# Second feed-forward opening block by block, activations stored in two groups, and down's activations loaded in five parts

## What is computed

```python
def _swiglu(u, w_gate, w_up, w_down):
    return (jax.nn.silu(u @ w_gate) * (u @ w_up)) @ w_down

h = x + 0.5 * _swiglu(_rms_norm(x, ffn1_norm), ffn1_w_gate, ffn1_w_up, ffn1_w_down)
...   # mixer, cross-attention
h = h + 0.5 * _swiglu(_rms_norm(h, ffn2_norm), ffn2_w_gate, ffn2_w_up, ffn2_w_down)
y = _rms_norm(h, final_norm)
```

## Time and profile before

| | |
|---|---|
| three runs | 2101.51, 2096.09, 2102.85 us, median 2101.51 |
| profiled execution | 2094.95 us |
| its span, from first to last instruction | 2093.2 us |
| TensorE matmul busy | 2038.1 us (97%) |
| VectorE, ScalarE, GpSimd busy | 1430.3 (68%), 634.3 (30%), 1230.0 us (59%) |
| mean granted TensorE clock | 0.993 |

### The profile page before, as it was taken

One profiled execution on the slowest core, in us unless ns is written; L12 is line 12 of the kernel. 1 busy time (PEld: TensorE's weight loads), 2 busy tenths in 40 slices (PEclk: granted clock), 3 DMA queues, 4 the chain that ended last, 5 costly groups with the idle time before them and its releaser, 6 DMA issues.

```text
span 2093.2 us, 24457 instructions
## 1 busy us (share of the span) xinstructions
PE 2038.1 (97%) x9194; PEld 1668.7 (80%) x9194; DVE 1430.3 (68%) x1602; ACT 634.3 (30%) x977; POOL 1230.0 (59%) x799
## 2 busy tenths in 40 slices
PE   8999999999999999999999999998999999999996
PEld 4887888888878787888877888787788888887885
DVE  7688867766777979653242555457777767787788
ACT  5422322333434500002121223234223223244452
POOL 6489988797545533122333421136799999984551
PEclk9999999999999999999999999999999999999998
DMA  7524233347776471422113241211223232268763
GB/s 267 172 76 142 105 139 112 129 172 268 262 263 215 130 185 61 118 80 67 51 50 121 84 139 51 102 40 60 76 101 106 96 125 85 93 231 282 262 227 129
DMA packets 140628, 286.37 MB, mean 137 GB/s; under 512 B 12384, under 2 KB 37600, under 8 KB 140128
## 3 DMA queue, kind: packets, MB, share of 16 engines
q1 hardware_dynamic: 100496, 233.21, 32.9%
q10 hardware_dynamic: 40016, 51.61, 7.6%
HBM read 222.39 MB, written 63.42 MB: 137 GB/s over the span
## 4 chain that ended last, share of the span: by engine, by line
PE 69%; DVE 19%; DMA 5%; issue 3%; POOL 2%; ACT 1%; SPq 1%; DVEq 0%; ACTq 0%
PE ps L528 66%; DMA raw<-in_dn 3%; DVE w_lo L2364 3%; DVE xt_lo L2354 2%; DVE f_g L1800 2%; DVE h L2373 2%; PE ps L853 1%; DMA d_act<-f_g 1%; DVE acc L1800 1%; PE ps L828 1%; DVE sq L2168 1%; DVE ua_lo L1800 1%; DVE ua_lo L1809 1%; POOL raw L1210 1%; DVE sq L2205 1%
## 5 line engine op out<-in xcount | busy, mean ns | idle before, releaser
L1144 POOL TENSOR_TENSOR w_lo<-raw,w_hi 128x512 fp32r<-128x512 f32 x352 | 559.5, 1609 | 177.9 <-ACT w_hi L1361 177.7
L528 PE MATMUL ps<-xt_hi,w_hi 128*128 128x512 f32 x1320 | 516.3, 391 | 8.2 <-DVE xt_lo L2354 7.6
L528 PE MATMUL ps<-xt_hi,w_lo 128*128 128x512 f32 x1320 | 513.8, 389 | 0.0
L528 PE MATMUL ps<-xt_lo,w_hi 128*128 128x512 f32 x1320 | 513.7, 389 | 0.0
L1361 ACT ACTIVATE w_hi<-raw 128x512 fp32r<-128x512 f32 x462 | 277.3, 625 | 494.2 <-POOL raw L1162 290.2
L1152 POOL TENSOR_SCALAR w_hi<-raw 128x1024 fp32r<-128x1024 f32 x54 | 61.9, 1147 | 471.7 <-PE ps L528 464.2
L528 PEld LDWEIGHTS ps<-xt_hi,w_hi 128*128 128x128 f32 x1320 | 247.8, 188 | 67.9 <-issue 14.7
L528 PEld LDWEIGHTS ps<-xt_hi,w_lo 128*128 128x128 f32 x1320 | 247.7, 188 | 51.8
L528 PEld LDWEIGHTS ps<-xt_lo,w_hi 128*128 128x128 f32 x1320 | 247.8, 188 | 50.6
L1162 POOL TENSOR_TENSOR raw<-raw 128x512 f32<-128x512 f32 x177 | 278.8, 1586 | 14.1 <-DMA raw<-in_gu 6.9
L1210 POOL TENSOR_TENSOR raw<-raw 128x512 f32<-128x512 f32 x110 | 165.1, 1512 | 140.9 <-DMA raw<-in_dn 140.8
(11 more groups left out here) (307 smaller groups left out, 2888.8 us busy)
## 6 DMA issues: line engine op xcount, KB each, us to landing
raw<-in_dn SPq DMA_DIRECT2D x264, 256.0 KB, 3.5
raw<-in_gu SPq DMA_DIRECT2D x88, 512.0 KB, 5.0
raw<-in_weights SPq DMA_DIRECT2D x54, 512.0 KB, 3.5
d_act<-acc SPq DMA_DIRECT2D x20, 512.0 KB, 2.8
d_act<-sq SPq DMA_DIRECT2D x20, 512.0 KB, 3.8
d_act<-f_g SPq DMA_DIRECT2D x20, 512.0 KB, 4.6
h<-in_x SPq DMA_DIRECT2D x16, 512.0 KB, 9.3
xt_hi<-d_act SPq DMA_DIRECT2D x8, 1024.0 KB, 7.7
```

The costliest lines, as they stand in the source:

```text
L528: ins = nc.tensor.matmul(out, lhsT, rhs, start=start, stop=stop)
L1144: add(lo, src, hi.bitcast(F32), op=ALU.subtract).then_inc(s_w_low["pool"], 1)
```

## The change

Three groups of edits.

- Opening of the second stage: `x_low` takes one part at a time, parts 0 and 1 of all four k-tiles first, then part 2; TensorE's passes of s4 come behind all of w11 and w12; VectorE adds the last two squares behind its first four bank adds; the sums of squares move from block 1 to block 3 of product 1; ScalarE's square root moves ahead of the copy of product 1.
- Stores: a new pair of semaphores. SyncE stores f_g's three blocks after `act_sum(2)` and the other four after `act_sum(4)`. ScalarE's copy waits for f_g's stores at even products and for the others at odd ones.
- Loads for down: `ACT_CHUNKS` has five parts of two blocks. SyncE issues them at every second step, from steps 6, 16, 26, 40 and 51 (before: every step from 16, 24, 34, 46 and 57). At step 6 and at step 16 it waits first until the last gate/up block is done.

```diff
-ACT_CHUNKS = ((0, 4), (4, 8), (8, 10))
+ACT_CHUNKS = ((0, 2), (2, 4), (4, 6), (6, 8), (8, 10))
...
-SUMS_AT, SPREAD_AT = (1, 1), (1, 6)
+SUMS_AT, SPREAD_AT = (1, 3), (1, 6)
...
                         for op in first[4:6]:
                             first_pass(op, kp)
-                        for k in ((), (0, 1), (2,), (3,))[kp]:
-                            first_pass(first[6], k)
+                    for kp in range(KP):
+                        pe.wait_ge(s_xb_lo, 2 * KP * 2 + kp + 1)
+                        first_pass(first[6], kp)
...
             def act_store(f, p):
 
+
+                two = lambda t: t.rearrange("p (c x) -> p c x", c=2)
+                sp.wait_ge(s_act_g, (FP - 1) * f + p + 1)
+                sp.dma_start(d_act[1:4:2, p].rearrange("c p x -> p c x"), two(f_g[:, 0])).then_inc(s_gstore, 16)
+                sp.dma_start(d_act[6, p], f_g[:, 1, 0:HALF]).then_inc(s_gstore, 16)
                 sp.wait_ge(s_act, FP * f + p + 1)
-                two = lambda t: t.rearrange("p (c x) -> p c x", c=2)
-                for x, to in ((two(acc[:]), d_act[0:3:2, p]), (two(sq[:]), d_act[4:6, p]), (two(f_g[:, 0]), d_act[1:4:2, p])):
+                for x, to in ((two(acc[:]), d_act[0:3:2, p]), (two(sq[:]), d_act[4:6, p])):
                     sp.dma_start(to.rearrange("c p x -> p c x"), x).then_inc(s_actst, 16)
-                sp.dma_start(d_act[6, p], f_g[:, 1, 0:HALF]).then_inc(s_actst, 16)
...
-                for s, first, emptied in ((2, 16, None), (3, 24, None), (4, 34, 0), (5, 46, 2), (6, 57, 3)):
-                    if d == first and emptied is not None:
+                for s, first, emptied in ((2, 6, None), (3, 16, None), (4, 26, 0), (5, 40, 2), (6, 51, 3)):
+                    if d == first and emptied is None:
+                        sp.wait_ge(s_gstep, GU_N * (f + 1))
+                    elif d == first:
                         sp.wait_ge(s_a_lo, DN_N * f + FP * (emptied + 1))
-                    if first <= d < first + len(ACT_CHUNKS):
-                        act_load(f, s, d - first)
+                    if first <= d < first + 2 * len(ACT_CHUNKS) and (d - first) % 2 == 0:
+                        act_load(f, s, (d - first) // 2)
...
                         if not combined_first(f, n) and i == (0 if n % 2 else 3):
-                            if n == 1:
-                                act.wait_ge(*((s_norm, 5) if f else (s_lastst, 32)))
+                            if f and n == 1:
+                                root()
+                                act.wait_ge(s_norm, 5)
+                            elif n == 1:
+                                act.wait_ge(s_lastst, 32)
                             elif n:
-                                act.wait_ge(s_actst, 64 * ((FP - 1) * f + n // 2))
+                                act.wait_ge(s_actst if n % 2 else s_gstore, 32 * ((FP - 1) * f + n // 2))
                             copy(F[0][:, C0], n, 0)
-                        if f == 1 and n == 1 and i == 1:
-                            root()
...
-                for at, s, c in ((1, 0, 0), (1, 0, 1), (2, 0, 2), (2, 1, 0), (7, 1, 1), (7, 1, 2)):
+                for at, s, c in ((1, 0, 0), (1, 0, 1), (1, 0, 2), (1, 0, 3), (2, 0, 4), (2, 1, 0), (2, 1, 1),
+                                 (7, 1, 2), (7, 1, 3), (7, 1, 4)):
                     if at == i:
                         act.wait_ge(s_gstep, last + i)
+                        act.wait_ge(s_gstore, 32 * (FP - 1) * (f + 1))
...
-                def x_low(k):
-                    for j in range(2):
-                        m = 2 * k + j
-                        dve.wait_ge(s_xb_hi, 2 * (KP * f + k) + j + 1)
-                        if j == 0:
-                            out, x, hi = xb_lo[:, 0, k], h[:, m, C0], xb_hi[:, 0, k]
-                        else:
-                            out, x, hi = xb_lo[:, 1:3, k], two(h[:, m]), xb_hi[:, 1:3, k]
-                        v.scalar_tensor_tensor(out=out, in0=x, scalar=gains[:, gi, m:m + 1], in1=hi.bitcast(F32),
-                                               op0=ALU.mult, op1=ALU.subtract).then_inc(s_xb_lo, 1)
+                def x_low(k, b):
+
+                    m, at = 2 * k + (b > 0), C1 if b == 2 else C0
+                    dve.wait_ge(s_xb_hi, 2 * (KP * f + k) + (b > 0) + 1)
+                    v.scalar_tensor_tensor(out=xb_lo[:, b, k], in0=h[:, m, at], scalar=gains[:, gi, m:m + 1],
+                                           in1=xb_hi[:, b, k].bitcast(F32), op0=ALU.mult, op1=ALU.subtract).then_inc(s_xb_lo, 1)
...
                     for k in range(KP):
-                        x_low(k)
+                        x_low(k, 0)
+                        x_low(k, 1)
+                    for k in range(KP):
+                        x_low(k, 2)
...
-                    add_squares(KT - 2)
-                    add_squares(KT - 1)
                     copied(0, 1)
                     op_done(0, 3)
...
                     add(F[0][:, C1], q["s1"], F[0][:, C1])
+                    add_squares(KT - 2)
+                    add_squares(KT - 1)
...
-                if k == 2:
-                    tt(acts_at(len(DN) - 1, FP - 1) if last else f_g[:, 1, C0], y[:, C0], y[:, C1], ALU.add)
+                if k == 2 and last:
+                    tt(acts_at(len(DN) - 1, FP - 1), y[:, C0], y[:, C1], ALU.add)
+                elif k == 2:
+                    v.tensor_tensor(f_g[:, 1, C0], y[:, C0], y[:, C1], ALU.add).then_inc(s_act_g, 1)
```

More of the change, by code:

```diff
@@ L361, in build @@
         s_diag, s_spread, s_rn = sem("diag_written"), sem("norm_spread"), sem("norm_kept")
-        s_gcopy, s_gadd, s_gate, s_silu, s_act, s_actst = (sem(n) for n in
-            ("gu_bank_copied", "gu_bank_added", "gate_scaled", "silu_written", "act_written", "act_stored"))
+        s_gcopy, s_gadd, s_gate, s_silu, s_act, s_actst, s_act_g, s_gstore = (sem(n) for n in
+            ("gu_bank_copied", "gu_bank_added", "gate_scaled", "silu_written", "act_written", "act_stored",
+             "act_in_gate_written", "act_in_gate_stored"))
         s_acts = [[sem(f"acts_loaded{b}_{c}") for c in range(len(ACT_CHUNKS))] for b in range(4)]
```

## The result

Four runs of the changed kernel took 2076.16 to 2079.00 us, median 2077.54; four of the kernel before beside them 2096.09 to 2102.85, median 2098.80. The ratio is 0.9895, with a 95% interval of 0.9878 to 0.9912: **21 us, 1.05% less**. The forecast was 2085, a gain of 15.1 us. The sign and the places were right. The gain of one part, the loads for down, was forecast at 5.5 us and is 11.1.

A forecast was written before the change was run, and what follows sets the result against it. The prediction took TensorE's matmul stream (97% busy) as the bound, with gains only at its waits and slow clock. Gains 2.4 + 7.2 + 5.5 = 15.1 us gave 2079.9; 5 added for a fast profiled execution made 2085, range 2077 to 2095.

The forecast's parts named there:

- 0.16 us more than its row says: TensorE's waits: each costs 0.16 us beyond its listed time, as the matmul before shows 0.39 us, not 0.23.
- Part C: Down stages: five spread loads remove most xt_lo waits; 5.5 us gained of 6.6, ends 0 and 6.6.
- gap in the weights: Down stages: 2.5 MB of activations issued in 5 us ahead of weights leave GpSimd waiting, 3.52 us at 1898.56.
- the longest of them would fall under 3 us: Sign in the down stages: GpSimd's waits for in_dn weights would be under 3 us.
- 289 GB/s is below what was carried: Down loads at every second step ask for 289 GB/s for 27 us, against 311 GB/s seen in the trace.
- Rival (1): Half-size loads for down don't carry, so their gain is 0; total gain 9.6 us, 2090; chance 0.10.
- the forecast's 164 and 238 GB/s: Loads for down: estimated rates of a half-size and a full-size load, from about 2 us fixed plus bytes.
- rival 4: Slower: SyncE waits at step 6 for gate/up's end, landing that weight over 7 us late; 2107, chance 0.03.
- Part B: Gate/up stages: separate stores of f_g end TensorE's waits for ScalarE's copy; 7.2 us gained, ends 5 and 8.5.
- Part A: Opening of the second gate/up stage: split low parts and reordered adds, sums and root; gain 2.4 us.
- the split's forecast price of 1.7 us: Opening of the second stage: splitting low parts by itself ends s4 1.7 us later, 1446.3 against 1444.6.
- if it isn't covered, 1 to 3 us: Behind the moved square root: ScalarE's late copy, block and load cost nothing, or 1 to 3 us if uncovered.

The follow-up runs named there:

- big_paced: Changed kernel with three loads for down instead of five, at the new first steps, one every fourth step; median 2079.9 us, down stages 209.43 and 211.54.
- big_early: Changed kernel with three loads for down instead of five, at the new first steps, one in every step; median 2079.9 us, down stages 210.97 and 212.93.
- five_double_late: Changed kernel with its five loads for down at the old first steps, two in each step; median 2081.6 us, down stages 214.39 and 211.97.
- five_dense_late: Changed kernel with its five loads for down at the old first steps, one in each step; median 2080.1 us, down stages 209.44 and 211.92.
- the control: Changed kernel with the loads for down undone (three parts, old first steps, every step); median 2089.0 us, down stages 216.29 and 216.15.
- B alone: Kernel before with only the stores in two groups added; median 2092.8 us, ratio to before 0.9955.
- B and C without A: Changed kernel with the opening of the second stage put back as before, new stores and loads for down kept; median 2081.1 us, ratio to before 0.9898.
- A alone: Kernel before with only the new opening of the second stage; median 2098.5 us, ratio to before 0.9987.
- low_unsplit: Changed kernel with the opening's low parts unsplit and s4's passes interleaved as before, the moved sums and root kept; median 2077.4 us, ratio to before 0.9881.

## Why the prediction was right and wrong, step by step

**What a wait costs.** The step "0.16 us more than its row says" was too low. TensorE's timeline of the changed kernel, a wait in the opening and the next matmul:

```profile
1431.56 0.50 PE L529 MATMUL ps<-xb_hi,w_hi 128*128 128x512 f32 x1 [0.71 <-DVE xb_lo L2101]
1431.90 0.40 PE L529 MATMUL ps<-xb_lo,w_hi 128*128 128x512 f32 x1
```

The first matmul behind a wait is followed after 0.34 us, not 0.23, so it is idle + 0.16 + 0.1, about 0.25. With that the seven waits of the first down stage of before give 4.4 us of idle time + 7 x 0.25 = 6.1, and a short one that the list leaves out makes it 6.3; the stage shrank by 6.5.

**Part C, the term that failed: 5.5 forecast, 11.1 measured** (6.5 in the first down stage and 4.6 in the second), outside the ends of 0 and 6.6 that were given. Three errors, all in sizing. I counted nine of the 15 waits as lying inside the down stages; all 15 do. Of the six left out, five of them late in the stages, four went too (two in the first stage, two in the second). I charged 0.16 for a wait, not 0.25. And I took 5.5 of 6.6 on the guess that VectorE's evacuation steps would keep some; they kept 0.4 us. The mechanism was right in its core, loads ahead of weights at too high a rate, and the "gap in the weights" shrank. GpSimd's waits for weights in the trace after and in the trace before (total, times, longest):

```profile
POOL raw L1216 <- DMA raw<-in_dn: 121.1, 84, 3.9
```
```profile
POOL raw L1210 <- DMA raw<-in_dn: 140.8, 74, 5.8
```

It still waits 121 us in all, and the forecast that the longest of them would fall under 3 us was wrong. Nor is it the longest that tells a good kernel from a bad one. The first row here is of big_paced, whose down stages are the shortest of all, the second of big_early, whose stages are 1.5 and 1.4 us longer:

```profile
POOL raw L1216 <- DMA raw<-in_dn: 120.0, 74, 5.2
```
```profile
POOL raw L1216 <- DMA raw<-in_dn: 130.7, 80, 4.7
```

The total goes with the stages: 119 to 124 us in the kernels that have the whole gain, 131 in big_early, 136 in five_double_late, 139 to 143 in those with the old loads. How much of such a gap ScalarE and VectorE can cover was not worked out. The bound "289 GB/s is below what was carried" was needlessly strict: 0.5 MB with each step, 385 GB/s by the same working, did no harm in five_dense_late, and the kernel before carried 389 GB/s in one stretch, the first 5 us of its second down stage (last two figures: DMA share and GB/s):

```profile
1858.00:1863.00 5.00, 5.00 (x24) 4.14 (x23) 4.83 (x5) 2.84 (x6) 4.20 (x4) 1.00 1.05 389
```

The rule of the Trainium skill (DMA: Bandwidth & Descriptors, section Bandwidth) that asks for batches of at least 1 MiB made no difference at the lower rates: five_dense_late and big_paced, at 0.5 and 1.0 MB a load, have down stages within 0.4 us. At the old rate the halves were better, not worse (five_double_late against the control). Rival (1), which rested on the rule, is out. The fit behind the forecast's 164 and 238 GB/s stands in another section of that page, Anatomy of one DMA — SWDGE (gpsimd) path, and both it and the rule's figures were measured on transfers that GpSimd issues, where these are SyncE's. My reading is that several transfers are in flight here at any time; that was not tested by itself.

**SyncE's stand at step 6 (rival 4)** was as worked out and cost nothing. SyncE's queue and TensorE's last gate/up matmul in the changed kernel, to set beside the earlier trace rows:

```profile
1847.35 0.39 PE L529 MATMUL ps<-xb_hi,w_lo 128*128 128x512 f32 x1
...
1847.77 0.38 SPq L1034 DMA_DIRECT2D xt_hi<-d_act  x1
1848.19 0.47 SPq L1128 DMA_DIRECT2D raw<-in_dn  x1
```

Step 6's weight goes out 0.8 us behind the last matmul instead of 4.1 ahead of it, and the list of TensorE's waits has none until far into the stage (2047 us). The stages with and without the stand (changed and five_dense_late) last equally long.

**Part B: 7.2 forecast, 2.2 + 5.1 = 7.3 measured alone.** The mechanism was right; that the number fits so well is partly luck. B alone lost 1.5 us to the slower sums ahead of the spread, which has no place in the working. Beside C it gave 2.2 + 6.6 = 8.8 us (before against B and C without A), 1.6 more than forecast and just over the upper end of 8.5. What the 7.2 left out are the two small waits for GpSimd's low parts (about 1.0 with their 0.25 each) and 0.1 for each of the three waits; and it took off 0.3 for a rest of the longest wait, which B and C without A does not have. The first store of the second stage, in the changed kernel, to set beside the earlier trace rows:

```profile
1482.36 0.69 DVE L2356 TENSOR_TENSOR f_g<-sq 128x512 f32<-128x512 f32 x1
1483.08 0.38 SPq L1024 DMA_DIRECT2D d_act<-f_g  x1
1483.50 0.47 SPq L1025 DMA_DIRECT2D d_act<-f_g  x1
...
1486.65 0.60 ACT L1462 ACTIVATE f_g<-ps 128x512 f32<-128x512 f32 x1 [12.57 <-DMA d_act<-f_g]
...
1487.30 0.50 PE L529 MATMUL ps<-xb_hi,w_hi 128*128 128x512 f32 x1 [0.38 <-ACT f_g L1462]
```

From issue to copy 3.6 us (3.8 forecast), and 0.38 us of the wait stay (up to 0.8 forecast). Over the run ScalarE waits 78.5 us for f_g's stores instead of 191.0, 3.9 each instead of 10. The three waits of TensorE for the copy are gone or nearly so, and with them the two of 0.18 and 0.35 us for GpSimd's low parts, 238 and 353 us into the second stage; the kernels without B have some of that kind there or at 124 us, those with B none. At the other places it gives nothing that the list of waits would show.

**Part A: 2.4 forecast; 3.2 at the spread, 1.4 net with B, 0.9 without.** That the order pays and the split doesn't was right; the split's forecast price of 1.7 us was wrong with the new order and too low (3.2) with the old one. I had put all four last low parts beside GpSimd at 1.7 us each, and the added work of the four more instructions at 0.4 to 1.1 us each; it was 14.8 less 13.2, so 0.4 each. VectorE's low parts in the changed kernel:

```profile
1434.45 0.74 DVE L2101 SCALAR_TENSOR_TENSOR xb_lo<-h,gains,xb_hi 128x512 fp32r<-128x512 f32 x1
...
1437.48 1.77 DVE L2101 SCALAR_TENSOR_TENSOR xb_lo<-h,gains,xb_hi 128x512 fp32r<-128x512 f32 x1
```

The ones between 1433.1 and 1436 took 0.74, in GpSimd's gap, and one of the last four fell into it, so they were done 1.6 us ahead of my layout. What I had missed is behind the spread: I took the gain there as kept. The step "if it isn't covered, 1 to 3 us" for ScalarE's late block was the place: TensorE waited 0.69 us for a low part of GpSimd's that it had not waited for before. I had also not worked out that without B the late store would take more of it: A alone is worth 0.9 us in its stage.

**The sum.** 2.4 + 7.2 + 5.5 = 15.1 forecast; in the changed kernel's stages 2.3 (B) + 8.0 (A and B) + 11.1 (C) + 0.4 (tail) = 21.8. Of the 6.7 us between, C is 5.6, B 1.6 too little and A 1.0 too much; 0.4 is the tail. The 5 us that I added for the profiled execution's being a fast one were right: its start was 2.4 to 7.4 us ahead of all others.

## What to carry to other kernels

Where a queue carries both urgent and patient loads, spread the patient ones, or issue them earlier. Here 0.5 MB with each step was enough, and then loads of 0.5 and of 1 MB did equally well; at 1 MB a step the smaller ones did better. Count the cost of a late operand as its idle time plus about a quarter of a microsecond, and count every wait with the same cause, also at the ends of a stage. Before crediting an earlier start of TensorE, follow it to the next thing that doesn't move with it (here a store): without moving that too, most of the gain was given back.

## What the runs showed of the hardware

After a wait of 4.84 us twelve 128 x 512 matmuls ran at the lower clock, and after one of 3.74 us eight; after five waits of 0.40 to 0.73 us within 12 us none did. Waits of the same length don't always do the same. In low_unsplit three waits of 0.89, 2.25 and 0.73 us in the opening were followed by no slow matmul. In B and C without A, after waits of 0.88 and 2.23 us, eight ran at the lower clock's 0.43 us spacing, the first 1.5 us after the second wait. In B alone and in before, with equal waits up to the sums of squares, the sums took 3.57 and 1.95 us. So the opening can differ by 1.5 us (49.02 against 47.51 up to the spread) with the same waits, by the clock. How long "between" lasts (700.1 to 703.2 us) varies from run to run of unchanged code, in part by the clock granted in it. VectorE's 512-column low part in the opening takes 0.74 us alone and 1.77 beside GpSimd's work in every kernel here (the first of them 1.27), about 1 us more whatever the width (1024 columns: 1.27 and 2.3), so splitting an instruction that runs beside GpSimd doubles the extra.
